# A recurrence kernel with three units in flight: the inversion of one unit is woven with the chunk steps of the unit before it

## The chip, the cores and the metric

The kernel runs on one core of a Trainium2 chip. The metric is the device time of one execution in microseconds (us). TensorE is called PE in the profile, VectorE DVE, ScalarE ACT, GpSimd POOL and SyncE SP.

## The reference

Two transformer-like blocks are computed one after the other on 256 tokens of width 2048, in float32. The first holds a state-space branch, a gated delta rule branch and a feed-forward network; the second windowed attention, an RWKV branch with a forward and a backward scan, and a feed-forward network. The change touches only the RWKV branch of the second block. Its core is this scan, run for 16 heads of 64, in both directions, first over 256 context tokens and then, from the final state, over the 256 latent tokens:

```
def wkv_scan(state0, r, w, k, v, kk, a, reverse):
    def step(S, inp):
        r_t, w_t, k_t, v_t, nkk_t, b_t = inp            # nkk = -kk, b = kk * a
        sa = jnp.einsum('bhvk,bhk->bhv', S, nkk_t)
        S = S * w_t[:, :, None, :] + sa[..., None] * b_t[:, :, None, :] + v_t[..., None] * k_t[:, :, None, :]
        return S, jnp.einsum('bhvk,bhk->bhv', S, r_t)
...
for d in range(2):
    Sc, yc_d = wkv_scan(S0, rc, wdc, kdc, vrc, kkc, adc, rev)
    _, y_d = wkv_scan(Sc, r, wd, kd, vr, kk, ad, rev)
    y_lat = y_lat + y_d
```

The sum of both directions is then normalised per head, a bonus term is added, and the result is gated.

## The kernel before, in words

The big projections outside the recurrence stream their weights through SBUF and split every float32 operand in a high and a low part. They are not changed.

The recurrence works on **units**. A unit is one pair of heads `j` (0 to 7) and one of two token sets: `c`, the context, or `l`, the latent tokens. There are 16 units in the order 0c, 0l, 1c, 1l, ... Both directions (`e` = 0 forward, 1 backward) of a unit are worked on together. A unit has three stages:

- **Preparation** (`prep_pe`, `prep_act`, `prep_dve`). Sigmoids of the decay and of `a`; for each direction a scan over tokens and three exponentials, then elementwise products (`k_bh`, `k_kh`, `k_ah`, and `k_rh` for `l`); transposes into `k_bk`; products of these per head ("heads"), which VectorE masks into `j_a`, `k_nt` and for `l` also `k_ab` and `k_ak`; `k_nv`; and the norm of the next unit's keys (`k_nrm`: sum, maximum, square root, reciprocal, product into `k_kk`).
- **Inversion.** The 64 by 64 unit triangular matrices `j_a` are inverted by doubling blocks. VectorE first writes three pairs of 128x512 tiles (`inv_first_dve`). Then follow five levels, each a mask step and a sum step: TensorE multiplies, VectorE masks the product (`inv_mask_*`), TensorE multiplies again, VectorE adds and transposes (`inv_sum_*`). Each step serves both directions.
- **Chunk steps** (`chunk_pe`, `chunk_act`, `chunk_dve`). The 256 tokens are four chunks of 64. For each chunk: TensorE reads the state (L1647) and VectorE subtracts it (`k_ur`, L1703); TensorE multiplies with the inverse (L1660) and ScalarE copies the result (`k_u`, L1689); TensorE makes the state update and, for `l`, the outputs (L1670 to L1678), and VectorE writes the new state (L1715, L1724). That makes 12 steps a unit.

After an `l` unit the **output stage** (`post_*`) normalises and gates the pair's result.

Each engine runs its own queue in the order in which the program is written, and semaphores tie the queues together. That order is made by Python generators: a stream (`prep`, `chunk`, `post`) yields after each of its steps, and `woven` takes a step of one stream and then a step of another. The same order is used on all three engines, so a step of one engine meets the same step of the others. Before, the inversion is the tail of the preparation's stream: a unit's stream has 18 stages (its last ten are the ten inversion steps) and the 12 chunk steps of the unit before it are taken after stages 0 to 7, 9, 11, 13 and 15. The loop over `j` makes seven passes, each with one `c` and one `l` unit; the rest stands ahead of the loop and behind it.

PSUM has eight banks, all used: `X` (two, state and output of the chunk steps), `I` (four, preparation and inversion) and `M` (two, sigmoids, `k_nv` and output stage).

Of the kernel before, what the change touches and what calls it, by code (L numbers as in the profile page):

```python
# [93 lines left out]
def program(nc, d):  # L94

    ctx = ExitStack()
    with ctx:
# [944 lines left out]
        j_a, k_nt, j_p = pair("j_a", [4, P], H0, 2), pair("k_nt", [4, P], H0 + 4, 2), pair("j_p", [4, P], H0 + 8, 2)  # L1042
# [40 lines left out]
        CHUNK_POINTS = (0, 1, 2, 3, 4, 5, 6, 7, 9, 11, 13, 15)  # L1083
# [9 lines left out]
        def lat(x, names):  # L1093
            return names if x == "l" else ""

        pre_p = {x: steps(f"pre_p_{x}", "s0 s1 a0 a1 vt bk0 bk1 hd0 hd1 im0 im1 nt0 nt1 " + lat(x, "ab0 ab1 ")
                          + "nv0 nv1 sum " + lat(x, "bonus kh0 kh1 ak0 ak1")) for x in "cl"}
# [3 lines left out]
                          + lat(x, "rh0 rh1 bo2 ") + "kq sq im0 im1 nt0 nt1 " + lat(x, "ab0 ab1 ") + "eps "  # L1101
                          + lat(x, "bv ak0 ak1 ") + "rec kk") for x in "cl"}
# [6 lines left out]
               else f"sa0_{s} sa1_{s} sb0_{s} sb1_{s}") for s in range(NCH))) for x in "cl"}  # L1109
# [6 lines left out]
        jinv = {x: [j_done[0] + ((j_a[0][:], j_work[0][:], j_inv[x][0][:], j_p[0][:]), (I[0], I[1]), "tt"),  # L1116
                    j_done[1] + ((j_a[1][:], j_inv[x][1][:], j_work[1][:], j_p[1][:]), (I[2], I[3]), "t")] for x in "cl"}
# [295 lines left out]
        def prep_pe(pe, j, x):  # L1413
# [3 lines left out]
            if x == "l":  # L1417
                pe.wait_ge(*pre_a["c"].at(j, "nv1"))
# [387 lines left out]
        def rk_pe(pe):  # L1806
            phases(pe, prep_pe, chunk_pe, post_pe)
# [648 lines left out]
```

## Time and profile before

| | |
|---|---|
| median of 3 runs | 4665.15 us (4664.57 to 4665.74) |
| profiled execution, its own time | 4663.12 us |
| span of that execution | 4661.4 us |
| TensorE, products | busy 4030.5 us (86%) |
| VectorE | busy 2571.5 us (55%) |
| ScalarE | busy 1670.2 us (36%) |
| recurrence, all 16 units and the last output stage | 931.9 us, from 2814.6 to 3746.5 |
| one pass of its loop (a `c` and an `l` unit) | 112.63 us |

The span is that of the instructions; the execution's own time is 1.7 us longer. Times in the views are microseconds from the start of the span, durations too unless marked ns. An instruction's row has its start, its duration, engine, line, operation, what it writes and reads, and in brackets how long its engine idled before it and who released it. A float32 product of TensorE appears as two instructions (x8 are four products).

### The profile page before, as it was taken

The numbers are of one execution on the slowest core, as the hardware profiler recorded it, in microseconds if no ns is written. First come the engines' busy times: TensorE is split into PE (matmuls) and PEld (weight loads), VectorE is DVE, ScalarE is ACT, GpSimd is POOL, SyncE is SP. The second block draws the span as 40 slices with busy tenths as digits, with TensorE's granted clock in tenths as the row PEclk, the third lists the DMA queues.
The fourth block names the chain that finished last, engine by engine and source line by source line (L and its number), as shares of the span: only waits on it lengthen the run. The fifth ranks groups of instructions, "written<-read, shape, count | busy, mean of one in ns | idle before, by whom it ended". The sixth has DMA issues, their size and how long they took to land.

```text
span 4661.4 us, 78517 instructions
## 1 busy us (share of the span) xinstructions
PE 4030.5 (86%) x29468; PEld 3621.7 (78%) x29468; DVE 2571.5 (55%) x4265; ACT 1670.2 (36%) x2326; POOL 23.7 (1%) x46
## 2 busy tenths in 40 slices
PE   7999777577999999998799646888888898999998
PEld 6999333355999999998689545776677788999998
DVE  3744776444647777544434335666766645444443
ACT  3545333212435555433213232222222135555433
POOL 0000000000000000000000000000000000000000
PEclk9999667666999999999899777888888889999999
DMA  4554666112444555554124000000000043555553
GB/s 159 180 187 176 230 232 264 59 51 89 175 163 153 181 183 185 171 181 153 63 99 144 34 0 11 3 2 2 2 2 2 1 168 142 185 181 180 172 183 123
DMA packets 80486, 568.08 MB, mean 122 GB/s; under 512 B 9472, under 2 KB 9728, under 8 KB 15520
## 3 DMA queue, kind: packets, MB, share of 16 engines
q1 hardware_dynamic: 78048, 558.50, 33.8%
q0 software_dynamic: 2368, 8.65, 0.5%
q8 instruction: 43, 0.70, 0.1%
q14 instruction: 27, 0.22, 0.0%
HBM read 565.02 MB, written 2.10 MB: 122 GB/s over the span
## 4 chain that ended last, share of the span: by engine, by line
PE 77%; DVE 13%; issue 5%; ACT 3%; DMA 1%; DVEq 1%; ACTq 0%; POOL 0%; SPq 0%; POOLq 0%
PE po L256 17%; PE po L257 17%; PE po L258 17%; PE po L1135 5%; PE pa L738 2%; PE po L814 2%; PE po L443 2%; PE pa L814 1%; PE pa L302 1%; PE po L738 1%; PE pa L1457 1%; PE po L1218 1%; DVE hf L313 1%; PE po L1226 1%; DVE j_work L852 0%
## 5 line engine op out<-in xcount | busy, mean ns | idle before, releaser
L244 DVE TENSOR_TENSOR w_lo<-raw,w_hi 128x1024 fp32r<-128x1024 f32 x880 | 1039.2, 1202 | 604.8 <-ACT w_hi L237 586.9
L256 PE MATMUL po<-hh,w_lo 128*128 128x256 f32 x4256 | 1207.0, 284 | 24.3 <-DVE hh L337 12.6
L257 PE MATMUL po<-hh,w_hi 128*128 128x256 f32 x4256 | 1206.4, 283 | 0.0
L258 PE MATMUL po<-hh,w_hi 128*128 128x256 f32 x4256 | 1206.3, 283 | 0.0
L237 ACT ACTIVATE w_hi<-raw 128x1024 fp32r<-128x1024 f32 (+1 forms) x877 | 898.4, 1038 | 804.4 <-PE po L258 621.6
L256 PEld LDWEIGHTS po<-hh,w_lo 128*128 128x128 f32 x4256 | 819.2, 192 | 25.6 <-issue 25.5
L257 PEld LDWEIGHTS po<-hh,w_hi 128*128 128x128 f32 x4256 | 819.3, 193 | 0.0
L258 PEld LDWEIGHTS po<-hh,w_hi 128*128 128x128 f32 x4256 | 819.1, 192 | 0.0
L256 PE MATMUL po<-f_hi,w_lo 128*128 128x256 f32 x1408 | 400.0, 284 | 6.2 <-DVE f_lo L1315 6.2
L257 PE MATMUL po<-f_lo,w_hi 128*128 128x256 f32 x1408 | 399.9, 284 | 0.0
L258 PE MATMUL po<-f_hi,w_hi 128*128 128x256 f32 x1408 | 399.8, 284 | 0.0
L256 PEld LDWEIGHTS po<-f_hi,w_lo 128*128 128x128 f32 x1408 | 271.7, 193 | 6.6 <-issue 6.6
L258 PEld LDWEIGHTS po<-f_hi,w_hi 128*128 128x128 f32 x1408 | 271.9, 193 | 0.0
L257 PEld LDWEIGHTS po<-f_lo,w_hi 128*128 128x128 f32 x1408 | 271.8, 193 | 0.0
L1135 PE MATMUL po<-hh,w_hi 128*128 128x512 f32 x704 | 218.4, 392 | 0.0
L1135 PEld LDWEIGHTS po<-hh,w_hi 128*128 128x128 f32 x704 | 133.5, 190 | 27.8
L1689 ACT ACTIVATE k_u<-pa 64x128 f32<-64x128 f32 x64 | 17.0, 265 | 378.3 <-PE po L1660 312.8
L1135 PE MATMUL po<-hh,w_lo 128*128 128x512 f32 x352 | 138.3, 393 | 15.9 <-DVE hh L337 15.9
L738 PE MATMUL pa<-j_work,j_a 128*128 128x128 f32 x640 | 106.9, 318 | 43.3 <-DVE j_work L826 43.3
L1289 ACT ACTIVATE f_hi<-conv_v 128x256 f32 x88 | 36.8, 418 | 278.3 <-DVE conv_v L1306 166.0
L738 PEld LDWEIGHTS pa<-j_work,j_a 128*128 128x128 f32 x640 | 90.5, 218 | 52.5 <-DVE j_work L826 46.0
L302 PE MATMUL pa<-hf,ones 128*128 128x256 f32 x224 | 60.9, 439 | 54.5 <-ACT hf L293 54.5
(539 smaller groups left out, 6501.3 us busy)
## 6 DMA issues: line engine op xcount, KB each, us to landing
raw<-ffn_up SPq DMA_DIRECT2D x176, 1024.0 KB, 4.8
raw<-w_in SPq DMA_DIRECT2D x112, 1024.0 KB, 4.8
raw<-ffn_down SPq DMA_DIRECT2D x64, 1024.0 KB, 4.9
raw<-ada SPq DMA_DIRECT2D x56, 1024.0 KB, 4.8
ada_buf<-ada SPq DMA_DIRECT2D x40, 1024.0 KB, 6.2
raw<-w_out SPq DMA_DIRECT2D x32, 1024.0 KB, 4.8
raw<-ffn_down SPq DMA_DIRECT2D x32, 768.0 KB, 4.2
raw<-glu SPq DMA_DIRECT2D x16, 1024.0 KB, 4.8
```

The lines of the kernel that those rows point to most:

```text
L237: act.activation(w_hi[:, k % 4, 0:width], raw[:, k // 2, (k % 2) * PW:(k % 2) * PW + width], ACT.Copy).then_inc(hi_ready, 1)
L244: dve.tensor_tensor(w_lo[:, k % 4, 0:width], raw[:, k // 2, (k % 2) * PW:(k % 2) * PW + width], w_hi[:, k % 4, 0:width].bitcast(F32), ALU. ...
L256: pe.matmul(po[bank][:, 0:T], lo, act_hi[:, t, :], start=first and n == 0, stop=False)
L257: pe.matmul(po[bank][:, 0:T], hi, act_lo[:, t, :], start=False, stop=False)
L258: mm = pe.matmul(po[bank][:, 0:T], hi, act_hi[:, t, :], start=False, stop=end)
L302: mm = pe.matmul(pa[0][:, 0:T], ones[:], hf[:, t, :], start=t == 0, stop=t == KD - 1)
L313: last = dve.scalar_tensor_tensor(out[:, t, :], x[:, t, :], w(t), rstd[:], ALU.mult, ALU.mult)
L443: mm = pe.matmul(po[m][32 * t:32 * t + 32, :], ada_vec[:, 4 * c + t, :], w[:, t * 512:t * 512 + 512], start=c == 0, stop=c == 3)
L738: mm = pe.matmul(out[:, m * P:m * P + P], lhs[:, m, :], ident[:] if rhs is None else rhs[:, m, :], start=True, stop=True)
L814: mm = pe.matmul(b[1][:, m * P:m * P + P].rearrange("p (a s) -> p a s", a=2), i_tt[:, m, :], i_p[:, m, 0:64].unsqueeze(1).broadcast_to([P, ...
L1135: mm = pe.matmul(po[o % 4][:].rearrange("p (s t) -> p s t", s=2), w, hh[:, ::-1, part, t, :], start=half == 0 and n == 0 and w is lo, stop ...
L1218: mm = pe.matmul(po[n][:, kb * P:kb * P + P], t_s[:, n, kb * P:kb * P + P], t_dg[:, n, :], start=True, stop=True)
```

## The change

The inversion becomes a stream of its own (`inverse_*`), and three units are in flight: while unit n does its chunk steps, unit n+1 is inverted and unit n+2 prepared. `woven` now takes its steps by one written list, `PERIOD`: V is an inversion step, C a chunk step, P a preparation step, O a step of the output stage. The inversion uses one bank per direction for mask and sum products (`inv_bank`, the former `M`); preparation has the four banks `I` to itself, for which its products for `k_ab` and `k_ak` are made one after the other instead of together; the output stage moves to the `X` banks. `j_a` and `j_p` move to parts of SBUF that hold split weights elsewhere in the kernel, so that they outlive the preparation.

```diff
-        j_a, k_nt, j_p = pair("j_a", [4, P], H0, 2), pair("k_nt", [4, P], H0 + 4, 2), pair("j_p", [4, P], H0 + 8, 2)
+        k_nt = pair("k_nt", [4, P], H0 + 8, 2)
+        j_a, j_p = pair("j_a", [4, P], 60, 2), pair("j_p", [4, P], 76, 2)
...
-        CHUNK_POINTS = (0, 1, 2, 3, 4, 5, 6, 7, 9, 11, 13, 15)
+        PERIOD = "V C V C C V C V C C V C V C C V C V C P C V P O V P O V P O P O P O P P P".split()
...
-        X, I, M = (pa[2], po[2]), (pa[0], pa[1], po[0], po[1]), (pa[3], po[3])
+        X, I, inv_bank = (pa[2], po[2]), (pa[0], po[0], pa[1], po[1]), (pa[3], po[3])
...
-        def woven(prep, chunk, post=None):
-            def step(stream):
+        def woven(**streams):
+
+            for turn in PERIOD:
+                stream = streams.get(turn)
                 if stream is not None:
                     next(stream, None)
-            for stage in range(18):
-                if stage in (0, 2, 3, 4, 6):
-                    step(post)
-                step(prep)
-                if stage in CHUNK_POINTS:
-                    step(chunk)
-
-        def phases(eng, prep, chunk, post):
-
-            woven(prep(eng, 0, "c"), None)
-            woven(prep(eng, 0, "l"), chunk(eng, 0, "c", False))
+
+        def phases(eng, prep, inverse, chunk, post):
+
+            woven(P=prep(eng, 0, "c"))
+            woven(V=inverse(eng, 0, "c"), P=prep(eng, 0, "l"))
             with eng.Fori(0, 7) as j:
-                woven(prep(eng, j + 1, "c"), chunk(eng, j, "l"))
-                woven(prep(eng, j + 1, "l"), chunk(eng, j + 1, "c"), post(eng, j))
-            woven(None, chunk(eng, 7, "l"))
-            woven(None, None, post(eng, 7))
+                woven(C=chunk(eng, j, "c"), V=inverse(eng, j, "l"), P=prep(eng, j + 1, "c"))
+                woven(C=chunk(eng, j, "l"), V=inverse(eng, j + 1, "c"), P=prep(eng, j + 1, "l"), O=post(eng, j))
+            woven(C=chunk(eng, 7, "c"), V=inverse(eng, 7, "l"))
+            woven(C=chunk(eng, 7, "l"), O=post(eng, 7))
...
-            pe.wait_ge(*V.at(j, "ab1" if x == "l" else "nt1"))
-            pe.wait_ge(*A.at(j, "a1"))
+            pe.wait_ge(*V.at(j, "nt1"))
             for e in range(2):
...
             if x == "l":
-                pe.matmul(I[3][:, 0:T], k_bd[:], k_bo[:], start=True, stop=True).then_inc(Q.did("bonus"), 1)
-                for e, mm in enumerate(heads(0, "ak", (I[0], I[2]), k_kh, k_rh)):
+                pe.wait_ge(*V.at(j, "rh1"))
+                for e, mm in enumerate(heads(0, I[0:2], k_bh, k_rh)):
+                    mm.then_inc(Q.did(f"bh{e}"), 1)
+                pe.wait_ge(*Q.at(j, "bh0"))
+                pe.wait_ge(*Q.at(j, "bh1"))
+                for e, mm in enumerate(heads(1, I[0:2], k_bh, k_rh)):
+                    mm.then_inc(Q.did(f"ab{e}"), 1)
+            yield
+            if x == "l":
+                pe.wait_ge(*V.at(j, "ab1"))
+                for e, mm in enumerate(heads(0, I[0:2], k_kh, k_rh)):
                     mm.then_inc(Q.did(f"kh{e}"), 1)
...
-            pe.wait_ge(*V.at(j, "ak1" if x == "l" else "eps"))
-            settle(pe)
-            for l in range(1, 6):
-                inv_mask_pe(pe, inv_no(j, x), jinv[x], l)
-                yield
-                inv_sum_pe(pe, inv_no(j, x), jinv[x], l)
-                yield
...
-            dve.wait_ge(*V.at(j, "im1"))
-            inv_first_dve(dve, inv_no(j, x), jinv[x], k_masks)
+            yield
             dve.wait_ge(*A.at(j, "sqrt"))
             then(dve.reciprocal(k_nrm[:], k_nrm[:]), "rec")
             signal(dve.tensor_tensor(k_kk[:, other], k_kk[:, other], k_nrm[:], ALU.mult), "kk")
+            yield
+
+        def inverse_pe(pe, j, x):
+            yield
+            pe.wait_ge(j_done[1][1], inv_no(j, x) * 17 + 3)
+            settle(pe)
+            for l in range(1, 6):
+                inv_mask_pe(pe, inv_no(j, x), jinv[x], l)
+                yield
+                inv_sum_pe(pe, inv_no(j, x), jinv[x], l)
+                yield
+
+        def inverse_dve(dve, j, x):
+            dve.wait_ge(*pre_v[x].at(j, "im1"))
+            inv_first_dve(dve, inv_no(j, x), jinv[x], k_masks)
             yield
```

The order on TensorE, at the start of the inversion of 0l, with the context unit's chunk steps beside it. L738 is a mask step and L814 a sum step of the inversion, two rows each (one per direction). Before:

```order
L738 MATMUL pa<-j_work_166,j_a_160 128x128 x4
L738 MATMUL po<-j_inv_l_171,j_a_161 128x128 x4
L814 MATMUL pa<-j_p_164,j_inv_l_170 128x128 x4
L814 MATMUL po<-j_p_165,j_work_167 128x128 x4
L1670 MATMUL pa<-k_u_201,k_bk_208 128x128
L1671 MATMUL pa<-k_vt,k_bk_208 128x128
L1670 MATMUL po<-k_u_202,k_bk_209 128x128
L1671 MATMUL po<-k_vt,k_bk_209 128x128
L738 MATMUL pa<-j_work_166,j_a_160 128x128 x4
L738 MATMUL po<-j_inv_l_171,j_a_161 128x128 x4
L814 MATMUL pa<-j_p_164,j_inv_l_170 128x128 x4
L814 MATMUL po<-j_p_165,j_work_167 128x128 x4
```

And now (L1668 is the former L1660, the product with the inverse; L1678 and L1679 are the state update; L1655 is the read of the state):

```order
L738 MATMUL pa<-j_work_166,j_a_162 128x128 x4
L738 MATMUL po<-j_inv_l_171,j_a_163 128x128 x4
...
L1668 MATMUL pa<-k_nv_c_172,j_inv_c_168 64x64 x2
...
L1668 MATMUL po<-k_nv_c_173,j_inv_c_169 64x64 x2
...
L1678 MATMUL pa<-k_u_201,k_bk_208 128x128
L1679 MATMUL pa<-k_vt,k_bk_208 128x128
...
L1678 MATMUL po<-k_u_202,k_bk_209 128x128
L1679 MATMUL po<-k_vt,k_bk_209 128x128
...
L814 MATMUL pa<-j_p_164,j_inv_l_170 128x128 x4
L814 MATMUL po<-j_p_165,j_work_167 128x128 x4
...
L1655 MATMUL pa<-k_S_205,k_ah_180 64x128
L1655 MATMUL po<-k_S_206,k_ah_181 64x128
```

Before, one chunk step stood behind every two inversion steps; now two chunk steps, of which the second needs ScalarE's copy of what the first made, stand between the mask step and the sum step.

The order on VectorE, from the end of a latent preparation into the inversion that follows. L1617 (now L1606) writes `k_ak`, L820 to L826 are `inv_first_dve`, L1622 (now L1614) is the reciprocal, L836 the mask of level 1. Before:

```order
L1617 TENSOR_TENSOR k_ak_212<-pa,k_masks 128x512
L1617 TENSOR_TENSOR k_ak_213<-po,k_masks 128x512
L1703 TENSOR_TENSOR k_ur_199<-k_nv_c_172,pa 64x128
L1703 TENSOR_TENSOR k_ur_200<-k_nv_c_173,po 64x128
L820 TENSOR_TENSOR j_inv_l_170<-j_a_160,k_masks 128x512
...
L826 STREAM_TRANSPOSE j_inv_l_171<-j_work_167 128x512
L1622 RECIPROCAL k_nrm<-k_nrm 128x256
L1623 TENSOR_TENSOR k_kk<-k_kk,k_nrm 128x256
L836 TENSOR_TENSOR j_p_164<-pa,k_masks 128x4x64
```

And now:

```order
L1606 TENSOR_TENSOR k_ak_212<-pa,k_masks 128x512
L1606 TENSOR_TENSOR k_ak_213<-po,k_masks 128x512
L1608 TENSOR_SCALAR k_nrm<-pa 128x256
L1611 TENSOR_TENSOR k_bv<-po,zkv 128x256
L1614 RECIPROCAL k_nrm<-k_nrm 128x256
L1615 TENSOR_TENSOR k_kk<-k_kk,k_nrm 128x256
...
L820 TENSOR_TENSOR j_inv_l_170<-j_a_162,k_masks 128x512
...
L826 STREAM_TRANSPOSE j_inv_l_171<-j_work_167 128x512
```

The reciprocal and the maximum ahead of it (L1608) moved from beside the first inversion products to a place ahead of the inversion's first instructions, and the inversion that follows is that of the unit prepared one period earlier.

## Rows read from the trace of the kernel before

**Rows 1.** Page, part 2 (granted clock in 40 slices) and part 5 (mean ns).
```profile
PEclk9999667666999999999899777888888889999999
...
L1689 ACT ACTIVATE k_u<-pa 64x128 f32<-64x128 f32 x64 | 17.0, 265 | 378.3 <-PE po L1660 312.8
```

**Rows 2.** Busy time by stretch: PE, PEld, DVE, ACT, POOL, then granted clock.
```profile
2814.60:3746.50 931.90, 751.45 (x5808) 638.58 (x5808) 630.16 (x1426) 205.49 (x465) 7.91 (x14) 0.81 0.01 2
3034.07:3146.70 112.63, 92.64 (x729) 78.97 (x728) 78.52 (x178) 25.62 (x58) 1.11 (x2) 0.83 0.01 2
3087.40:3120.04 32.64, 22.08 (x152) 16.63 (x150) 24.63 (x56) 12.74 (x28) 1.11 (x2) 0.71 0.03 8
3709.30:3746.50 37.20, 27.73 (x160) 20.12 (x160) 10.67 (x28) 3.65 (x12) 0.00 (x0) 0.54 0.00 1
```

**Rows 3.** Waits of PE, one pass: total us, times, longest.
```profile
PE pa L738 <- DVE j_work L826: 5.3, 2, 2.6
PE pa L1437 <- DVE k_kh L1571: 3.9, 1, 3.9
```

**Rows 4.** Timeline of PE: inversion steps, one state read between them.
```profile
3068.42 1.16 PE L738 MATMUL pa<-j_work,j_a 128*128 128x128 f32 x8
3070.31 1.06 PE L814 MATMUL pa<-j_p,j_inv_c 128*128 128x128 f32 x8
3072.19 0.32 PE L1647 MATMUL pa<-k_S,k_ah 128*64 128x128 f32 x1
3072.56 1.16 PE L738 MATMUL pa<-j_work,j_a 128*128 128x128 f32 x8
```

**Rows 5.** Timeline: first scans of preparations, first inversion products.
```profile
3036.12 0.69 DVE L1563 TENSOR_TENSOR_SCAN k_cs<-k_rst,k_s 128x256 f32<-128x256 f32 x1 [0.51 <-ACT k_s L1516]
3060.46 2.08 PE L738 MATMUL pa<-j_work,j_a 128*128 128x128 f32 x8 [2.65 <-DVE j_work L826]
3089.36 0.69 DVE L1563 TENSOR_TENSOR_SCAN k_cs<-k_rst,k_s 128x256 f32<-128x256 f32 x1 [1.97 <-ACT k_s L1516]
3120.04 0.80 PE L738 MATMUL pa<-j_work,j_a 128*128 128x128 f32 x2 [2.65 <-DVE j_work L826]
```

**Rows 6.** Timeline of PE: state update begins; what follows the slow one.
```profile
3065.64 0.37 PE L1670 MATMUL pa<-k_u,k_bk 64*128 64x128 f32 x1
3041.08 0.58 PE L1670 MATMUL pa<-k_u,k_bk 64*128 64x128 f32 x1
3045.87 0.69 PE L1437 MATMUL po<-ident,k_bh 128*128 128x128 f32 x2
```

**Rows 7.** Timeline of DVE: one direction's preparation; start of an inversion.
```profile
3094.26 0.68 DVE L1563 TENSOR_TENSOR_SCAN k_cs<-k_rst,k_s 128x256 f32<-128x256 f32 x1
3097.63 0.48 DVE L1576 SCALAR_TENSOR_TENSOR k_x<-k_kd,par,zr 128x256 f32<-128x256 f32 x1
...
3116.87 0.69 DVE L820 TENSOR_TENSOR j_inv_l<-j_a,k_masks 128x512 f32<-128x512 f32 x1
3119.91 0.67 DVE L826 STREAM_TRANSPOSE j_inv_l<-j_work 128x512 f32<-128x512 f32 x1
3120.51 1.71 DVE L1622 RECIPROCAL k_nrm<-k_nrm 128x256 f32<-128x256 f32 x1
3122.25 0.43 DVE L1623 TENSOR_TENSOR k_kk<-k_kk,k_nrm 128x256 f32<-128x256 f32 x1
```

**Rows 8.** Timeline of PE and ACT: products for k_nv, a table load.
```profile
3053.77 1.10 PE L1482 MATMUL pa<-k_vt,k_nt 128*128 128x64 f32 x8
3055.60 0.65 PE L1486 MATMUL pa<-k_nrm,k_bd 128*128 128x256 f32 x2
3056.20 1.28 ACT L1537 ACT_TABLE_LOAD   x1
```

**Rows 9.** Busy time by stretch, three microseconds each, around a rise.
```profile
3040.00:3043.00 3.00, 2.96 (x12) 2.30 (x14) 2.77 (x7) 1.76 (x5) 0.00 (x0) 0.50 0.00 0
3049.00:3052.00 3.00, 3.00 (x39) 2.52 (x37) 1.09 (x2) 0.54 (x2) 0.00 (x0) 0.87 0.00 0
```

More of the change, by code:

```diff
@@ L1458, in heads @@
                 return mm
-            for name, bank, w, m in products_of:
-                if name == "ab":
-                    pe.wait_ge(*A.at(j, "a1"))
-                    if x == "l" and not (isinstance(j, int) and j == 0):
-                        pe.wait_ge(*po_v.at(j - 1, "eps"))
-                        pe.wait_ge(*po_a.at(j - 1, "gt"))
-                mm = heads(0, name, bank, w, m)
-            for e in range(2):
-                mm[e].then_inc(Q.did(f"hd{e}"), 1)
+            pe.wait_ge(*V.at(j, "ah1"))
+            pe.wait_ge(*A.at(j, "a1"))
+            heads(0, I[0:2], (k_bh[0], k_ah[1]), (k_ah[0], k_bh[1]))
+            pe.wait_ge(*A.at(j, "bk1"))
+            for e, mm in enumerate(heads(0, I[2:4], k_kh, k_ah)):
+                mm.then_inc(Q.did(f"hd{e}"), 1)
             yield
@@ L1471, in prep_pe @@
             pe.wait_ge(*Q.at(j, "hd1"))
-            for name, bank, w, m in products_of:
-                for e, mm in enumerate(heads(1, name, bank, w, m)):
-                    mm.then_inc(Q.did(f"{name}{e}"), 1)
+            for e, mm in enumerate(heads(1, I[0:2], (k_bh[0], k_ah[1]), (k_ah[0], k_bh[1]))):
+                mm.then_inc(Q.did(f"im{e}"), 1)
+            for e, mm in enumerate(heads(1, I[2:4], k_kh, k_ah)):
+                mm.then_inc(Q.did(f"nt{e}"), 1)
             yield
-            pe.wait_ge(*V.at(j, "ab1" if x == "l" else "nt1"))
-            pe.wait_ge(*A.at(j, "a1"))
+            pe.wait_ge(*V.at(j, "nt1"))
             for e in range(2):
@@ L1492, in prep_pe @@
                 pe.wait_ge(*Q.at(j, "kh1"))
-                for e, mm in enumerate(heads(1, "ak", (I[0], I[2]), k_kh, k_rh)):
+                for e, mm in enumerate(heads(1, I[0:2], k_kh, k_rh)):
                     mm.then_inc(Q.did(f"ak{e}"), 1)
+            pe.wait_ge(*V.at(j, "sq"))
+            pe.wait_ge(*A.at(j, "nv0"))
+            pe.matmul(I[2][:, 0:T], k_bd[:], k_nrm[:], start=True, stop=True).then_inc(Q.did("sum"), 1)
+            if x == "l":
+                pe.wait_ge(*A.at(j, "nv1"))
+                pe.matmul(I[3][:, 0:T], k_bd[:], k_bo[:], start=True, stop=True).then_inc(Q.did("bonus"), 1)
             yield
             yield
-            pe.wait_ge(*V.at(j, "ak1" if x == "l" else "eps"))
-            settle(pe)
-            for l in range(1, 6):
-                inv_mask_pe(pe, inv_no(j, x), jinv[x], l)
-                yield
-                inv_sum_pe(pe, inv_no(j, x), jinv[x], l)
-                yield
         def prep_act(act, j, x):
@@ L1534, in prep_act @@
                 act.wait_ge(*Q.at(j, f"nv{e}"))
-                act.activation(k_nv[x][e][:], two(M[e]), ACT.Copy).then_inc(A.did(f"nv{e}"), 1)
+                act.activation(k_nv[x][e][:], two(I[2 + e]), ACT.Copy).then_inc(A.did(f"nv{e}"), 1)
+            yield
             act.wait_ge(*V.at(j, "eps"))
@@ L1606, in prep_dve @@
                     dve.wait_ge(*Q.at(j, f"ab{e}"))
-                    signal(dve.tensor_tensor(k_ab[e][:], quarters(M[e]), bc4(k_masks[:, m:m + 1, :]), ALU.mult), f"ab{e}")
+                    signal(dve.tensor_tensor(k_ab[e][:], quarters(I[e]), bc4(k_masks[:, m:m + 1, :]), ALU.mult), f"ab{e}")
             yield
+            if x == "l":
+                for e in range(2):
+                    m = 7 + 2 * e
+                    dve.wait_ge(*Q.at(j, f"ak{e}"))
+                    signal(dve.tensor_tensor(k_ak[e][:], quarters(I[e]), bc4(k_masks[:, m:m + 1, :]), ALU.mult), f"ak{e}")
             dve.wait_ge(*Q.at(j, "sum"))
-            signal(dve.tensor_scalar(k_nrm[:], I[1][:, 0:T], 1e-12, None, ALU.max), "eps")
+            signal(dve.tensor_scalar(k_nrm[:], I[2][:, 0:T], 1e-12, None, ALU.max), "eps")
             if x == "l":
```

90 lines of the change are left out of this document (38 added, 52 removed).

## The prediction

> **What bounds the kernel now.** I read the page first, then the recurrence cut into stretches, then TensorE's waits in one pass of its loop, then the timeline of that pass. On the page the reader sees the granted clock fall to 0.7 or 0.8 in the middle third and return to 0.9 around it [rows 1]. That third holds the recurrence: 931.9 us, TensorE busy 751 us of them and VectorE 630, almost no transfers [rows 2]. The loop makes seven equal passes of 112.6 us, so 788 us are in the loop and 143.5 outside it. In a pass TensorE is busy for 92.6 us and VectorE for 78.5, with TensorE's clock at 0.83 [rows 2]. Neither is full, so the order in which the in-order engines meet each other is the bound. TensorE's longest waits are for the first masks of an inversion (5.3 us in two waits) and for `k_kh` early in a preparation (3.9 us) [rows 3]. After such a wait it runs at half clock: the first eight products of an inversion take 2.08 us after 2.65 us of idling and 1.16 us later on [rows 4, 5].
>
> The first scan of each preparation and the first product of each inversion cut a pass into four parts [rows 5]: context preparation 24.3 us (3036.12 to 3060.46), inversion 28.9, latent preparation 30.7, inversion 28.6. Half of every chunk recurrence hides in a preparation and half in an inversion.
>
> **The change, part by part.** The amount of work is the same. What changes is which two streams share an engine's queue. Now a whole recurrence (12 steps) is woven with the inversion, and the preparation follows with nearly nothing beside it except the last inversion steps and, in the latent half, the output steps. I replay the new order with the durations of the trace, all at the upper clock.
>
> *Weave in the context half.* An inversion step takes TensorE 1.9 us (3068.42 to 3070.31, both directions) and a state read 0.37 [rows 4]. The solve step takes the same 0.4; the two `k_u` copies of ScalarE (265 ns and a like one) that the next step waits for take 0.6 with the hops [rows 1]. The state update of a context chunk is 0.65 (the first half of the latent one). Read, mask step, solve, copy, update and sum step give 0.4 + 1.85 + 0.4 + 0.6 + 0.65 + 1.85, and 0.1 to 0.25 because `k_ur` stands behind two transposes on VectorE: 5.9 us a level. First mask, solve, copy and update 3.5; three levels 17.6; the sigmoid products in the place of a copy 0.5; the fourth sum and its transposes 3.5. Together **25.1 us** to the first scan.
>
> *Weave in the latent half.* The update is 2.8 us here (3065.64 to 3068.42) [rows 4, 6], the last one 1.4, so 3.5 becomes 5.6, a level 8.05, the whole **32.4 us**. Before, an inversion had five chunk steps beside it and one or two updates; now it has all four, each with the wait for ScalarE in front of it, because two chunk steps stand back to back.
>
> *Preparation in the context half.* First direction 3.55 us and second 3.2 up to `k_kh` (a latent one takes 3.85, 3094.26 to 3098.11) [rows 7]. The fifth mask, now between them, 1.05. Transposes 0.55, their copy 0.65, products 1.15. Four masks of the width of 3116.87 to 3118.1, 2.6 [rows 7]. Products for `k_nv` 1.85 (3053.77 to 3055.60) and the norm's sum 0.6 [rows 8]. Then 0.45 for the maximum and 1.05 for the square root, most of its table load of 1.28 us being uncovered [rows 8]. Reciprocal and product 2.15 (1.71 + 0.43) and the six first instructions of the inversion 3.7 (3116.87 to 3120.58) [rows 7]. Sum **22.6 us**. The reciprocal is the one piece that was hidden and now is not: it ran while TensorE worked on the first mask, and now stands ahead of the inversion's start.
>
> *Preparation in the latent half.* Two directions 7.7, fifth mask 1.05, last sum 0.85, y work 0.85 (three short operations), `k_rh` to squares 1.85, the output's variance, root, reciprocal and product 3.1: 15.4. Masks 2.6. Then `k_nv` 1.85, `k_ab` products and masks 2.3, `k_ak` 2.3, norm 0.9, reciprocal 2.15, inversion 3.7: 13.2. Sum **31.2 us**.
>
> A pass is 25.1 + 22.6 + 32.4 + 31.2 = 111.3 us, all at the upper clock. The 112.6 of before hold half-clock stretches as well, so this is no gain yet.
>
> *The clock.* TensorE now idles from the norm's sum to the first mask, about 7 us (0.45 + 1.05 + 2.15 + 3.7), twice a pass; 2.65 us sufficed before [rows 5]. It also idles about 2.5 us before the first transposes and 2.2 to 5.3 before `k_nv`. What lies on the path at half speed costs: first mask and what follows it 2.5 in the context half, 3.5 in the latent (longer update); in the context tail 3.8 (products 1.8, `k_nv` and sum 2.0); in the latent tail 6.4 (output products and fifth sum 2.0, `k_nv`, `k_ab`, `k_ak` and sums 4.4). All of it is 16.2 us. In the latent preparation of before a clock of 0.71 means 58% of the time at the lower level [rows 2], and dense work does bring it back: from 0.50 at 3040 to 0.87 at 3049 [rows 9]. Between 0.58 and 1 I take 0.8, since the new tails are thinner: 13.0. So a pass takes **124.3 us** (120.7 to 127.5).
>
> *A rule beside it.* By the Trainium skill (TensorE: Matmul & The Clock Gate, section Loop structure matters more than you think), bursts of products parted by long waits run at the cold clock, every one. This speaks against the change. By that rule all 16.2 us would be paid, by the trace's 0.8 of them 13.0; the trace agrees on inversion starts [rows 5] and disagrees inside preparations [rows 9].
>
> *Outside the loop.* To the first inversion product of the loop: preparation alone 26.6 (an estimate: the 24.3 of [rows 5] and 2.3 for the lower clock throughout) and 2.15 for the reciprocal; inversion of four levels with the sigmoids 19.2; transposes 1.8; a latent tail without output work 27.3; lower clock 4: 81.0. After it: weave, fifth level and its clock 31, then the last latent recurrence and output as now, 37.2 [rows 2]. Together 149.2 against 143.5: +5.7.
>
> *The two banks and moved tiles.* Mask and sum product of one direction share a bank, but each already waits for VectorE's read of the other, so I cost this at nothing; without that cover it would be one hop, 0.1 us, per step. `j_a` and `j_p` lie where no piece of weights is held ahead, also nothing.
>
> Sum against the profiled execution: 4663.1 + 7 x (124.3 - 112.6) + 5.7 = 4751. The median of the runs stands 2.0 above the profiled one, hence **4753 us**.
>
> **The rivals.** *The main case*, tails and starts mostly at half clock: 4753, its own range 4715 to 4790.
> *Only inversion starts are slow*: 2 x 1.9 on 111.3 gives 115.1 a pass and 4688. For: preparations before regained the clock. Against: their TensorE work had a chunk recurrence beside it.
> *The clock never falls*: the denser weave holds the upper level through the tails. 111.3 a pass, no 6.5 outside: 4655, faster or no change. It decides once half speed costs under 1.4 us a pass. Against it stand the waits of 7 us.
> *The clock falls inside the latent weave*: solve, copy and update make 3.8 us of chunk work alone. Chunk steps with nothing beside them run at 0.54 [rows 2], and an update at half speed took 4.8 us (3041.08 to 3045.87) [rows 6]. Three updates and three sums: 11.7 more, 136.0 a pass, 4835.
> *Every burst is slow*: 127.5 a pass, 4775. This is what the skill's page named above would give.
>
> **How the numbers follow.** Chances: main 0.44, starts only 0.16, never falls 0.14, falls in the weave 0.14, every burst 0.12. The range goes from 4670 to 4835, leaving out the never-falls case and the upper part of the weave case. A change under 0.2% (9 us) is about what a measurement of this kernel can't tell from none. The never-falls case is 0.10 faster and 0.04 same; I add 0.02 to faster for hops counted too long: faster 0.12, same 0.04, slower 0.84.
>
> **What would show it.** Passes of 120.7 to 127.5 us; TensorE's wait for the first mask of an inversion near 7 us, twice a pass, after the norm's sum; a wait before `k_nv` near 5 us in the latent half, with VectorE at the output's reciprocal; a first mask step of about 3.5 us; levels of 5.9 and 8.05 us; clock in the loop below 0.83. I am wrong if the weave levels cost no more than 5.2 us, if TensorE finds preparation work ready during the weave, or if the clock stays up in the tails.

## The result, and the profile after

The changed kernel takes 4781.32 us (median of 4 runs, 4779.84 to 4783.34), the one before 4665.44 us (4664.57 to 4667.67): 1.0248 times as long, 95% interval 1.0230 to 1.0266. The prediction was 4753 us, slower, with a range of 4670 to 4835. The loss was forecast at 88 us and is 116; between the two profiled executions it is 120.

First the page: its first and second part, and from its fifth the group of the inversion's mask steps (busy us, mean ns, idle time of TensorE just before them and the releaser of most of it). The last line is that group in the kernel before.

```profile
PE 4068.1 (85%) x29468; PEld 3649.9 (76%) x29468; DVE 2570.6 (54%) x4265; ACT 1673.4 (35%) x2326; POOL 23.3 (0%) x46
...
PEclk9999666668999999997998778777787789999999
...
L738 PE MATMUL pa<-j_work,j_a 128*128 128x128 f32 x640 | 105.0, 315 | 120.8 <-DVE j_inv_l L826 67.5
```

```profile
L738 PE MATMUL pa<-j_work,j_a 128*128 128x128 f32 x640 | 106.9, 318 | 43.3 <-DVE j_work L826 43.3
```

VectorE is as busy as before; only the same work stands wider apart. TensorE's 38 us more of busy time are the same products at a lower clock. Against [rows 1] the recurrence (slices 25 to 32 of the clock's line) reads mostly 7 where it read mostly 8, and TensorE idles 120.8 us ahead of the mask steps instead of 43.3.

The steady passes of the loop take 129.5 to 129.8 us instead of 112.6. Cut at the first scan of each preparation and the first mask step of each inversion, one pass reads so (busy time of PE, PEld, DVE, ACT, POOL, then the granted clock; compare [rows 2]):

```profile
3054.92:3184.72 129.80, 97.21 (x728) 82.99 (x727) 78.36 (x180) 26.07 (x59) 1.07 (x2) 0.79 0.01 2
3054.92:3079.51 24.59, 12.46 (x82) 9.97 (x81) 17.65 (x37) 6.19 (x13) 0.00 (x0) 0.71 0.00 0
3079.51:3116.50 36.99, 36.08 (x300) 31.86 (x301) 16.88 (x46) 6.34 (x15) 0.00 (x0) 0.87 0.00 0
3116.50:3156.76 40.26, 21.62 (x120) 16.66 (x119) 26.81 (x54) 7.43 (x17) 1.07 (x2) 0.67 0.02 7
3156.76:3184.72 27.96, 27.05 (x228) 24.50 (x229) 17.02 (x46) 6.12 (x15) 0.00 (x0) 0.92 0.00 0
```

The reader is to see two kinds of stretch. In the weaves (third and fifth row) TensorE is busy 97% of the time and VectorE 46 and 61%; in the preparations (second and fourth) TensorE is busy 51 and 54% and VectorE 72 and 67%. The engines take turns to wait for each other. Of the 17.2 us that this pass is longer than that of [rows 2], TensorE idles 12.6 (32.6 us against 20.0), and 4.6 are the same products taking longer (97.2 us against 92.6). TensorE's waits in that pass (total us, times, longest), against [rows 3]:

```profile
PE pa L738 <- DVE j_inv_l L826: 9.2, 1, 9.2
PE pa L738 <- DVE j_inv_c L826: 6.6, 1, 6.6
PE pa L1472 <- DVE k_nt L1594: 5.7, 2, 3.5
PE po L1436 <- DVE k_kh L1564: 5.7, 2, 2.9
PE pa L1678 <- ACT k_u L1697: 1.8, 6, 0.3
PE pa L1450 <- DVE k_ab L1600: 1.4, 1, 1.4
```

The waits for the first mask were 2.65 us each and are 6.6 and 9.2. Why the second is longer stands in the timeline of VectorE and TensorE at the end of the pass (start, duration, in brackets the idle time and its releaser):

```profile
3149.70 0.42 DVE L1615 TENSOR_TENSOR k_kk<-k_kk,k_nrm 128x256 f32<-128x256 f32 x1
3152.90 0.69 DVE L820 TENSOR_TENSOR j_inv_l<-j_a,k_masks 128x512 f32<-128x512 f32 x1 [2.78 <-issue]
3156.76 2.05 PE L738 MATMUL pa<-j_work,j_a 128*128 128x128 f32 x8 [9.22 <-DVE j_inv_l L826]
```

L1615 is VectorE's last instruction of the loop's body and L820 its first. Between them it does nothing for 2.78 us, and the profile names no releaser. This comes at each of the six turns of the loop, 2.56 to 2.78 us long, and the prediction has nothing of it. In the kernel before the same turn lies between an inversion's last sum and the next preparation, and costs VectorE 0.13 us:

```profile
3033.11 0.42 DVE L848 TENSOR_TENSOR j_inv_l<-po,j_inv_l 128x256 f32<-128x256 f32 x1 [0.47 <-PE po L814]
3033.66 0.29 DVE L1558 COPY k_vs<-zkv 128x256 f32 x1
```

Last, TensorE in the latent weave of the same pass: mask steps (L738) and sum steps (L814) of context inversion, with eight instructions per direction (pa is the first).

```profile
3079.51 2.05 PE L738 MATMUL pa<-j_work,j_a 128*128 128x128 f32 x8 [6.57 <-DVE j_inv_c L826]
3086.81 2.07 PE L814 MATMUL pa<-j_p,j_inv_c 128*128 128x128 f32 x8
3090.38 1.16 PE L738 MATMUL pa<-j_work,j_a 128*128 128x128 f32 x8
3095.94 1.86 PE L814 MATMUL pa<-j_p,j_inv_c 128*128 128x128 f32 x8
3097.59 1.91 PE L814 MATMUL po<-j_p,j_work 128*128 128x128 f32 x8
3099.87 1.16 PE L738 MATMUL pa<-j_work,j_a 128*128 128x128 f32 x8
3105.43 1.16 PE L814 MATMUL pa<-j_p,j_inv_c 128*128 128x128 f32 x8
3107.79 1.16 PE L738 MATMUL pa<-j_work,j_a 128*128 128x128 f32 x8
```

From one mask step to the next the levels take 10.9, 9.5 and 7.9 us. The first starts at half clock (2.05 against 1.16). In the second the mask step is fast again and the sum step at 3095.94 slow again, though TensorE had no wait longer than 0.35 us between them. The third is fast throughout.

The half clock at the start was there before the wait of 6.57 us, which begins at 3072.94. This is the stretch ahead of it, TensorE busy throughout and the granted clock 0.50:

```profile
3069.00:3072.00 3.00, 3.00 (x14) 2.59 (x13) 0.00 (x0) 0.97 (x3) 0.00 (x0) 0.50 0.00 0
```

### The profile page after: what moved, and what is told of

Read it like the earlier page. It is cut to its first block, busy times and chain, and to the rows that moved or that the text cites. A ratio compares the mean times of both kernels' runs of the same rounds, so it can differ in the third digit from the quotient of the medians.

```text
span 4781.7 us, 78407 instructions
## 1 busy us (share of the span) xinstructions
PE 4068.1 (85%) x29468; PEld 3649.9 (76%) x29468; DVE 2570.6 (54%) x4265; ACT 1673.4 (35%) x2326; POOL 23.3 (0%) x46
## 4 chain that ended last, share of the span: by engine, by line
PE 78%; DVE 12%; issue 5%; ACT 3%; DMA 1%; DVEq 1%; ACTq 0%; POOL 0%; SPq 0%; POOLq 0%
PE po L256 16%; PE po L258 16%; PE po L257 16%; PE po L1136 5%; PE pa L738 3%; PE po L814 2%; PE pa L814 2%; PE po L738 2%; PE po L443 2%; PE pa L302 1%; PE pa L1450 1%; PE po L1219 1%; DVE hf L313 1%; DVE k_nrm L1614 1%; PE po L1472 1%
## 5 line engine op out<-in xcount | busy, mean ns | idle before, releaser
L256 PE MATMUL po<-hh,w_lo 128*128 128x256 f32 x4256 | 1207.5, 284 | 24.3 <-DVE hh L337 12.6
L256 PEld LDWEIGHTS po<-hh,w_lo 128*128 128x128 f32 x4256 | 819.4, 193 | 25.6 <-issue 25.5
L738 PE MATMUL pa<-j_work,j_a 128*128 128x128 f32 x640 | 105.0, 315 | 120.8 <-DVE j_inv_l L826 67.5
L738 PEld LDWEIGHTS pa<-j_work,j_a 128*128 128x128 f32 x640 | 90.5, 219 | 137.4 <-DVE j_work L826 129.5
```

The costliest lines, as they stand in the source:

```text
L256: pe.matmul(po[bank][:, 0:T], lo, act_hi[:, t, :], start=first and n == 0, stop=False)
L738: mm = pe.matmul(out[:, m * P:m * P + P], lhs[:, m, :], ident[:] if rhs is None else rhs[:, m, :], start=True, stop=True)
```

## The experiments

The main theory: the loss is what stands uncovered on VectorE at the two seams between a preparation and the next weave (norm's maximum, root, reciprocal and product, turn of the loop, six first instructions), and the half clock that this wait brings. The rivals: the weaves themselves, with two chunk steps back to back, are the loss; the shared banks are; or the clock falls by the weave's own products. Runs of different batches are compared by the ratio to the kernel before, or the text says that it takes the medians. That kernel's own runs in these batches lie between 4654 and 4676 us, so differences under some 10 us are not read. "A pass" is the mean over six passes of the profiled execution, from the first scan of a latent preparation to that of the next: 112.6 us before, 129.7 after.

**1. The reciprocal behind the inversion's first instructions.**

```diff
-PERIOD = "V C V C C ...
+PERIOD = "V K C V C C ...        # K: norm of the unit prepared in the period before
-            dve.wait_ge(*A.at(j, "sqrt"))                  # in prep_dve, last step
-            then(dve.reciprocal(k_nrm[:], k_nrm[:]), "rec")
-            signal(dve.tensor_tensor(k_kk[:, other], ...), "kk")
+        def kknorm_dve(dve, j, x):                         # the same three lines, taken at K
```

> Only change against the changed kernel: the reciprocal and the product into k_kk stand behind the six first instructions of the next inversion on VectorE, as before. Main theory (what stands uncovered on VectorE at the two seams is paid in full): the first mask product starts 2.8 us earlier in the context half (reciprocal 1.74, product 0.43, its wait 0.76) and 2.1 us earlier in the latent half, 4.9 us a pass, 34 us in all, so 4747 us; TensorE's waits ahead of the first mask fall from 6.6 and 9.2 us to about 3.8 and 7.0. Rival (the seams are bound by something else, the weaves set the time): within 9 us of 4781.

Measured: 4750.83 us, ratio 1.0197 (1.0175 to 1.0218), less than the changed kernel by 30 us by the medians and by 24 us by the ratios; a pass 126.3. TensorE's waits:

```profile
3187.51 2.05 PE L738 MATMUL pa<-j_work,j_a 128*128 128x128 f32 x8 [3.72 <-DVE j_inv_c L826]
3263.21 2.05 PE L738 MATMUL pa<-j_work,j_a 128*128 128x128 f32 x8 [6.85 <-DVE j_inv_l L826]
```

6.57 has become 3.72 and 9.2 has become 6.85, as the main theory says. The two preparations got shorter by 2.4 and 2.0 us, and the latent weave longer by 1.5 (38.5 us against 37.0), so a pass gains 3.4 us and not 4.9. The inversion still starts at half clock after 3.72 us.

**2. The first instructions early, in VectorE's hole.**

```diff
-PERIOD = "... P O P O P P P"
+PERIOD = "... P O P F O P P P"    # F: inv_first_dve of the unit being prepared
```

> Against the changed kernel, the six first instructions of an inversion stand right behind the masks of j_a and k_nt of the preparation that makes its j_a, in VectorE's hole while TensorE makes k_nv. Main theory: TensorE goes on from the norm's sum to the first mask with hardly a wait; 7.2 us less in the context half, 7 in the latent half (TensorE then waits for the end of its own products), and one or two more from a clock that idles less: 14 to 17 us a pass, 4662 to 4683 us, which is the time of the kernel before or nearly. Rival (TensorE's weaves at about 6 and 8 to 9.5 us a level are the loss, the seams are incidental): less than 7 us a pass, over 4730 us.

Measured: 4665.29 us, ratio 0.9999 (0.9989 to 1.0008); a pass 115.3. The time is that of the kernel before, with the three units in flight, the weaves and the banks as they are in the changed kernel. The preparations shrink from 24.6 to 17.6 us and from 40.2 to 31.1, and the weaves do not (37.1 and 29.5 us against 37.0 and 27.9). That decides between the theories: the waits at the seams were the bulk of the loss. A pass is still 2.7 us longer than before; outside the six passes the recurrence is 12 us shorter. The edit takes more off TensorE's wait than the 3.7 us of the moved instructions: the maximum, root, reciprocal and product no longer stand ahead of them either. All waits of TensorE over 1.5 us in a pass are now these, none of them for a first mask, except a sum of six short ones for `k_u` (2.0 us):

```profile
PE pa L1472 <- DVE k_nt L1594: 5.7, 2, 3.5
PE po L1436 <- DVE k_kh L1564: 5.7, 2, 2.9
PE pa L814 <- DVE j_p L836: 2.0, 1, 2.0
```

The clock's part of the loss did not go with the waits. This is the pass, and the start of its context inversion:

```profile
3136.07:3251.81 115.74, 96.77 (x728) 82.88 (x727) 78.06 (x179) 26.09 (x59) 1.07 (x2) 0.82 0.01 3
3153.40 2.08 PE L738 MATMUL pa<-j_work,j_a 128*128 128x128 f32 x8
```

TensorE's products take 96.8 us, nearly the 97.2 of the changed kernel (92.6 before), while its idle time fell from 32.6 us to 19.0. The context inversion starts at half clock with no wait at all ahead of it (so do five of the loop's seven); the last wait was one of 2.19 us, for the `k_nt` masks, 4 us earlier. The latent inversions do start faster without the wait (first mask step of both directions 2.0 to 2.3 us against 3.75). But over five passes the products take only 1.1 us a pass less than in the changed kernel (96.1 against 97.2). So "the half clock that this wait brings" in the main theory is a small part at most: the saving is the waits.

The third wait of the list is the turn of the loop again, which now meets VectorE ahead of the mask of level 1:

```profile
3222.15 1.25 PE L738 MATMUL pa<-j_work,j_a 128*128 128x128 f32 x8
...
3227.51 0.42 DVE L836 TENSOR_TENSOR j_p<-pa,k_masks 128x256 f32<-128x256 f32 x1 [2.58 <-issue]
```

**3. The loop written out.**

```diff
-            with eng.Fori(0, 7) as j:
+            for j in range(7):
```

> The loop over j is written out, seven copies with constant j; nothing else differs from the changed kernel. Main theory: the 2.6 to 2.8 us which VectorE spends between the last instruction of a pass and the first of the next, with the profile naming no releaser, is the turn of the loop, and it stands on the path since TensorE waits there 9.2 us instead of 6.6: six or seven turns, 17 to 19 us less, 4763 us, and both waits of a pass near 6.6. Rival: that time is the fetch of instructions or something that stays with straight code: 4775 to 4790 us, waits unchanged.

Measured: 4760.81 us, ratio 1.0212 (1.0194 to 1.0230), less than the changed kernel by 20.5 us by the medians and by 17 by the ratios; a pass 126.3. VectorE at the same place, and TensorE behind it:

```profile
3268.87 0.42 DVE L1615 TENSOR_TENSOR k_kk<-k_kk,k_nrm 128x256 f32<-128x256 f32 x1
3269.21 0.68 DVE L820 TENSOR_TENSOR j_inv_l<-j_a,k_masks 128x512 f32<-128x512 f32 x1
3273.20 2.04 PE L738 MATMUL pa<-j_work,j_a 128*128 128x128 f32 x8 [6.49 <-DVE j_inv_l L826]
```

The gap is gone, both waits of a pass are near 6.5 us, and the latent preparation takes 37.3 us instead of 40.2. The gap comes with the hardware loop and goes with it. Run 7 comes back to what fills it.

**4. Idle products in the waits for the first mask.**

```diff
+        def filler_pe(pe, j, x):      # taken after the last P; first waits for the inversion before
+            for n in range(16 if x == "c" else 20):
+                pe.matmul(inv_bank[0][:, 0:P], k_bd[:], k_bd[:], start=True, stop=True)
```

> TensorE makes 16 (context) and 20 (latent) idle products of 128x128 into an inversion bank while it waits for the first mask; their results are overwritten unread. It leaves nothing out. Clock theory: the first mask product then runs at the upper clock, 2.05 us instead of 3.5 and 3.8, the latent levels 1 and 2 take 8 us instead of 10.9 and 9.5, and a pass shortens by about 6 us: 4739 us. Rival 1: the latent weave slows itself, its second level stays at 9.5 us: 2 to 3 us a pass, 4763 us. Rival 2: fillers at half clock last longer than the wait and hold TensorE up: slower than 4781 us.

Measured: 4765.97 us (4747.77 to 4772.12), ratio 1.0206 (1.0180 to 1.0232), but a pass of 129.8, as without them. Ahead of the latent inversions the 20 products lasted 5 us and left 3.8 to 4.8 us of waiting in the loop, and the mask step stayed slow; so the run doesn't test the theory there. Ahead of the context inversions 16 products left 1.6 to 2.7 us. After 1.60 to 2.23 us of waiting (five of the loop's seven) the start was at the upper clock, after 2.69 and 2.73 it was not. This one had the fastest first level:

```profile
3327.86 1.13 PE L738 MATMUL pa<-j_work,j_a 128*128 128x128 f32 x8 [1.60 <-DVE j_inv_c L826]
3333.39 1.16 PE L814 MATMUL pa<-j_p,j_inv_c 128*128 128x128 f32 x8
3335.74 1.16 PE L738 MATMUL pa<-j_work,j_a 128*128 128x128 f32 x8
3341.45 2.07 PE L814 MATMUL pa<-j_p,j_inv_c 128*128 128x128 f32 x8
3345.23 1.16 PE L738 MATMUL pa<-j_work,j_a 128*128 128x128 f32 x8
3350.79 1.63 PE L814 MATMUL pa<-j_p,j_inv_c 128*128 128x128 f32 x8
3354.68 1.16 PE L738 MATMUL pa<-j_work,j_a 128*128 128x128 f32 x8
```

Level 1 takes 7.9 us here instead of 10.9. But levels 2 and 3 take 9.5 and 9.45, and level 3 took 7.9: the clock falls in the sum steps of the latent weave after a fast start too. That is rival 1. Of the 3.0 us that the fast start gave, 1.5 were given back two levels later.

**5. The kernel before with one bank per direction.**

```diff
-(j_inv..., j_p[0][:]), (I[0], I[1]), "tt"),  ... (I[2], I[3]), "t")
+(j_inv..., j_p[0][:]), (I[0], I[0]), "tt"),  ... (I[2], I[2]), "t")
```

> The kernel before with one change of the two banks alone: mask and sum product of a direction share a bank in the inversion. If the shared bank costs nothing, as forecast, because each product already waits for VectorE's read of the other: 4665 us, within 9. If it adds a hop of 0.1 us to each of ten steps of 16 inversions: 4681 us. If the changed kernel's loss came from the banks: over 4700 us.

Measured: 4664.40 us, ratio 0.9997 (0.9986 to 1.0007). The shared bank costs nothing. The moved tiles `j_a` and `j_p` were not tried apart; run 2 has both edits, and its total is that of the kernel before.

**6. Runs 2 and 3 together.**

> The early first instructions (as in the second run) and the loop written out (as in the third) together. In the trace of the second run VectorE still spends 2.6 us at the turn of the loop, and TensorE waits 1.97 us there for the mask of level 1. If the turn costs what TensorE waits, about 2 to 2.8 us in six or seven passes: 12 to 19 us less than 4665, 4646 to 4653 us, faster than both kernels. If the clock takes the time back: within 9 us of 4665.

Measured: 4632.83 us, ratio 0.9941 (0.9924 to 0.9958); a pass 111.2. Faster than both kernels, and by 27 us more than run 2 (0.0058 of 4665) where 12 to 19 were forecast. With the turn, the first level of a latent inversion took 9.0 us (3222.15 to 3231.11 in run 2), here 6.6 (3215.88 to 3222.45). The forecast counted the wait alone. In five passes of each trace TensorE idles 18.7 us a pass here against 19.2 in run 2, since other waits grew, and its products take 92.6 us against 96.1: the gain shows up as a higher granted clock.

**7. Control: the kernel before with its loop written out.**

> Control: the kernel before with its loop written out. Its turn lies inside the weave of output stage and preparation, where TensorE's 2.1 us ahead of the output stage's first product is off the chain and VectorE idles for ScalarE's sigmoids anyway. Main theory (the turn became a cost through the new order): within 9 us of 4665. Rival (the turn costs the same in either order, and is no part of the difference): 4646 us.

Measured: 4669.24 us, ratio 1.0014 (1.0000 to 1.0027). Not faster: the turn is a cost of the new order alone. In the profiled execution three of six passes, cut at the first scan of the context preparation, are as long as before (112.6 us) and three longer (115.3 to 117.3), so writing the loop out has an effect of its own, which was not followed up. The expectation puts the turn at the wrong place, though. The row of `k_vs` shown above is where it is, with 0.13 us of idling, and with the loop written out that idling is gone. TensorE's 2.1 us lie half a pass later and are no turn: written out, TensorE still idles there, 2.36 us.

What differs at the turn stands in the view of the DMA queues (packets, MB, share). From 3030 to 3700 the kernel before moves no instruction packet at all. The changed kernel moves 26 in the same stretch (first line); one of them starts inside VectorE's gap in each of its six turns, and in each of run 2's six (second line: the gap from 3150.12 to 3152.90).

```profile
q14 instruction: 26, 0.21, 0.1%
q14 instruction: 1, 0.01, 0.7%
```

So the loop of the new order loads instructions anew in every pass, and the old one runs without loading any, though VectorE has as many instructions in it (334 to 338 a pass, its sequencer's included, against 336). Written out, the new order still moves instruction packets, none of them in the stretch at 3269 of run 3. That VectorE waits for this load is the likely reading of the gap; why the old loop needs none no run shows.

**8. Idle products inside the latent weave of the changed kernel.**

```diff
+                if x == "l" and not end:           # behind the solve step
+                    for n in range(3):
+                        pe.matmul(I[0][:, 0:P], k_bd[:], k_bd[:], start=True, stop=True)
```

> The changed kernel with three idle products of 128x128 behind each latent solve step of TensorE but the last, into a bank that is free there; nothing is left out. They take 0.83 us at the upper clock, some 0.35 of it in TensorE's wait for ScalarE's copy: 0.5 us each, 1.4 us a pass if the clock does nothing else. Theory that the latent weave's own run of small update products lets the clock fall: with larger products among them the second level's sum step stays at 2.05 us instead of 3.56, and a pass is about even, 4781 us within 10. Rival (the fall comes from the wait ahead of the inversion, whose effect arrives late): the sum steps stay slow, and the time is 4790 to 4800 us.

Measured: 4771.56 us, ratio 1.0234 (1.0207 to 1.0262); a pass 129.7, even. Sum steps now:

```profile
3332.24 2.05 PE L738 MATMUL pa<-j_work,j_a 128*128 128x128 f32 x8 [6.57 <-DVE j_inv_c L826]
3340.58 1.16 PE L814 MATMUL pa<-j_p,j_inv_c 128*128 128x128 f32 x8
3349.07 1.16 PE L814 MATMUL pa<-j_p,j_inv_c 128*128 128x128 f32 x8
3357.43 1.16 PE L814 MATMUL pa<-j_p,j_inv_c 128*128 128x128 f32 x8
```

The start is as slow as ever and every sum step of the latent weave is fast, where the first, second and fifth were slow (3.3, 3.6 and 3.5 us for both directions against 2.05). So the second fall of the clock is the weave's own, and not an echo of the wait ahead of it. In its place the first sum step of the context weave became slow (3.3 to 3.4 us), which had been fast: the slow stretch moved.

**9. The output stage's reciprocal behind the masks (on run 6).**

```diff
-PERIOD = "... P O P O P F O P P P"
+PERIOD = "... P O P P F O O P P P"
```

> Against the sixth run: the output stage's root, reciprocal and product of VectorE stand behind the masks of j_a and k_nt and the inversion's first instructions, in the time in which VectorE waits for the products of k_ab, where the reciprocal stood ahead of the masks. TensorE's wait ahead of the k_nv products of the latent half should fall from 3.4 to about 2.1 us (the masks then wait for their own products), 1.3 us a pass and 9 us in all: 4624 us. If VectorE's 2.2 us come back ahead of the masks of k_ab: within 5 us of the sixth run, 4633.

Measured: 4642.63 us, ratio 0.9965 (0.9952 to 0.9977); a pass 112.0. The wait for the `k_nt` masks fell as said, from 3.4 to 2.2 us, and TensorE's wait for the masks of `k_ab` rose from 1.3 to 3.0. The 2.2 us of VectorE came back there; nothing is won.

**10. The scan one inversion step earlier (on run 9).**

```diff
-PERIOD = "... P C V P O V P O V P O P P F O O P P P"
+PERIOD = "... P C P V O P V O P V O P P F O O P P P"
```

> As the ninth run, and the first direction's scan and the k_kh transposes stand one inversion step earlier, so that TensorE's wait for k_kh (2.7 us twice a pass) is shorter. If that wait is on the path: 1.5 us twice a pass, about 20 us less than the ninth run, 4604 us. If VectorE's chain of the preparation is the bound and the inversion steps are merely later: within 9 us of the ninth run.

Measured: 4633.72 us, ratio 0.9949 (0.9932 to 0.9965); a pass 109.6. 9 us less than run 9 and level with run 6; some 20 were forecast if the wait is on the path, and under 9 if it is not. TensorE's waits for `k_kh` add up to 6.7 to 8.2 us a pass here and to 5.5 to 6.8 in run 9: they grew. The wait for `k_ab` differs from pass to pass, 2.2 to 4.7 us here against 2.0 to 3.1. That VectorE's chain of the preparation bounds this part is the likely reason, and was not tried apart.

**11. One idle product behind the solve step (on run 6).**

> The sixth run with one idle product of 128x128 (0.28 us) behind each direction pair's latent solve step but the last, inside TensorE's 0.35 us wait for ScalarE. If one larger product in that place is enough to hold the clock, two slow sum steps of 3.5 us a pass become 2.05, 1.5 to 2.9 us a pass, 10 to 20 us less: 4618 us. If it takes three as in the eighth run: the same as the sixth, 4633 us within 9.

Measured: 4644.69 us (4628.09 to 4658.49), ratio 0.9956 (0.9943 to 0.9970); a pass 112.7. TensorE no longer waits for ScalarE in the latent weave, yet the first sum step is slow (first row; the second, in the other row, is fast, and the third and fifth are slow again):

```profile
3275.86 2.07 PE L814 MATMUL pa<-j_p,j_inv_c 128*128 128x128 f32 x8
3285.70 1.16 PE L814 MATMUL pa<-j_p,j_inv_c 128*128 128x128 f32 x8
```

So it is not the 0.35 us gap that lets the clock fall there. With three idle products behind each solve step it stayed up in the latent weave and with one it did not; what about the run of small update products between them makes it fall was not isolated.

**12. Three idle products (on run 10).**

> The tenth run with three idle products of 128x128 behind each latent solve step but the last, the number that kept the clock up in the eighth run (one did not, in the eleventh, though it filled TensorE's wait for ScalarE). In the tenth run two or three sum steps of a latent weave take 3.3 to 3.5 us. If they become 2.05: 2.9 to 4.4 us less a pass against 1.5 us of idle products, 10 to 20 us less in all, 4614 to 4624 us, with passes that no longer differ. If the clock drops elsewhere instead: 4634 us within 9, or slower by the 10 us of the idle products.

Measured: 4633.31 us, ratio 0.9941 (0.9927 to 0.9954); a pass 109.0. All sum steps of the latent weaves are fast, and the passes are nearly even (108.5 to 109.5 from one latent inversion to the next), and the time is that of run 10. The idle products cost about what the clock gives back.

## Why the prediction was right in kind and 28 us short

- **Mechanism.** Right on the waits. The forecast named the reciprocal, the first instructions and the maximum and root as newly uncovered on VectorE, with TensorE's wait of about 7 us twice a pass. Run 2 takes them out of that wait and 14.4 of the 17.1 us a pass go; run 1 takes the reciprocal and its product alone out and gets 24 to 30 us, where 34 were worked out.
- **The parts.** With the clock terms as forecast, 25.6, 35.2, 36.3 and 27.1 us were to be found (context preparation, latent weave, latent preparation, context weave). Measured: 24.6, 37.0, 40.3, 28.0. Context levels behind the first took 6.07 us for 5.9, and the latent level without a slow step 7.9 for 8.05. The first mask and its pair took 3.5 and 3.8 us for 3.5. The wait before `k_nv` in the latent half was 3.5 us, where one near 5 was named as a sign.
- **The step that failed: TensorE's wait "about 7 us" in both halves.** It is the sum of VectorE's instructions and holds no turn of the loop. In the new order the turn falls between L1615 and L820, on the path: 9.2 us instead of 6.6, 2.7 us in six turns, 16 us; run 3 finds 17 by the ratios and 20.5 by the medians. The Trainium skill (Runtime: NRT & Kernel Launch, section Instruction fetch mechanics) says that a taken branch to code outside the prefetched part stalls for a fetch. The traces agree: a gap of 2.6 to 2.8 us with an instruction packet in it, gone when the loop is written out, and 0.13 us with no packet in the kernel before. Which loops pay it could not be told from the prediction's rows.
- **The clock's term, the second step that was too small.** Forecast as 0.8 of 16.2 us, 13.0 a pass. Against the parts at the upper clock (22.6, 32.4, 31.2, 25.1) the measured ones are longer by 2.0, 4.6, 9.1 and 2.9 us, 18.5 in all. Less 2.8 for the turn that leaves 15.7, if all of it is the clock's. In the tail of the latent preparation, from 3134 to 3146, the granted clock was 0.50 (1.00 from 3128 to 3134); that term was 6.4 whole and not 0.8 of it (9.1 - 2.8 = 6.3). That the number came so near is in part luck: the forecast ties the half clock at the starts to the wait of 7 us, and run 2 has no such wait and nearly the same product time (96.1 us a pass against 97.2, 92.6 before).
- **The rival of the clock falling in the latent weave** was true in small: of the three full levels the first two have a slow sum step, 1.2 and 1.5 us more each (3.3 and 3.6 against 2.05), instead of three updates and three sums at 11.7. Runs 4, 8 and 11 show it apart from the start, and in run 11 the first level took 12.4 us.
- **Outside the loop** +5.7 was forecast. The recurrence is 120.6 us longer in the profiled executions (928.0 to 1048.6 from its first scan), and its loop 116.5 of them (788.5 to 905.0), so it is about +4.
- **Banks.** Right, by run 5, for the shared bank. A pass came out at 129.8, over the 127.5 that was the forecast's upper end. The loop alone was forecast 35 us too short (81.9 for 116.5); that the total is only 28 short is because the rest was forecast some 2 us too long and the median lies 2.0 us below the profiled execution, where it was put 2.0 above.
- **A misreading that costs nothing.** The rows x8 of an inversion's start, called eight products, are eight instructions and so four products.

The rule of the Trainium skill named in the prediction (TensorE: Matmul & The Clock Gate, section Loop structure matters more than you think) gave 4775 us and lay nearest. It agrees with the traces where a long wait stands: every inversion start after 3.72 us or more of waiting was slow. It doesn't cover the context starts of run 2, which are slow without a wait just ahead of them, nor the latent weave, where no wait stands ahead of the slow sum steps.

## What to carry to other kernels

When work is split into stages that follow each other on in-order engines, look at the seam first: list what the one engine must still do between the other's last product and its next, and put what depends on early results (here the first instructions of the inversion, whose input is there 9 and 19 us sooner) into a hole that the engine has anyway. That one move was worth 116 us. The deeper weaving brought nothing as long as the turn of the loop was in it, and 0.6% without (run 6). Whether the same move would help the kernel before, where TensorE waits 2.65 us for each first mask, was not tried. Look also at where the turn of a loop falls: it cost nothing in one order and 17 to 27 us in the other. Idle products to hold the clock left the passes as long as they were (129.8 and 129.7 us against 129.7, 109.0 against 109.6); the medians of runs 4 and 8 are 15 and 10 us lower, which is at the edge of what is read here.

## What the runs showed of the hardware

- The turn of the loop leaves VectorE idle for 2.53 to 2.87 us in the new orders (the changed kernel and runs 1, 2, 4 and 8) and for 0.10 to 0.13 us in the kernel before. In the changed kernel and in run 2 an instruction packet of 8 KB starts inside each of these gaps; in the kernel before the loop moves no instruction packet from 3030 to 3700.
- TensorE's granted clock fell to about half in a stretch in which it was always busy (changed kernel, the second sum step of the latent weave):

```profile
3095.94:3099.50 3.56, 3.56 (x21) 3.34 (x20) 1.30 (x4) 0.00 (x0) 0.00 (x0) 0.54 0.00 0
```

It follows a latent chunk's update, many products of 64 columns or rows. Beside context chunks, whose update is short, the clock is 1.00 over three levels (3164.77 to 3183.18). With three products of 128x128 ahead of each update (run 8) the sum steps of the latent weave were fast; with one (run 11) they were not.
- The passes of one execution need not be alike: 109.2 to 113.3 us in run 6 and 113.1 to 116.0 in run 2, but 129.5 to 129.8 in the changed kernel. Which steps are slow shifts from pass to pass.
- Waiting is not needed for a slow start: in run 2 five of the loop's seven context inversions begin at half clock with no idle time ahead (2.08 us for the eight instructions at 3153.40).
